# State space layer of a two-block model: where power zero of the output matrices comes from, and which engine flips the coefficients

## The reference, cut to what matters

```python
def s5_mixer(xn, w_in, lam_re, lam_im, b_re, b_im, c_re, c_im, d_skip, log_dt, w_glu):
    u = xn @ w_in                                  # 512 x 1024, in 64 groups of 16
    lam, dt = complex(lam_re, lam_im), exp(log_dt)[:, None]
    a_bar = exp(lam * dt)                          # (64 groups, 64 states)
    b_bar = ((a_bar - 1.0) / lam)[..., None] * complex(b_re, b_im)
    c_mat = complex(c_re, c_im)                    # (64 groups, 16 outputs, 64 states)
    # for every group: s[t] = a_bar * s[t-1] + b_bar @ u[t];  y[t] = real(c_mat @ s[t])
    y = y + d_skip * u
    g = gelu(y)
    val, gate = split(g @ w_glu, 2)
    return val * sigmoid(gate)
```

## Time and profile before

| | us |
|---|---|
| median of 3 runs | 2036.3 (2035.78 to 2037.21) |
| profiled execution, its own time | 2034.78 |
| its span in the trace | 2033.0 |
| PE busy | 1966.4 (97%) |
| DVE busy | 1381.4 (68%) |
| ACT busy | 865.5 (43%) |
| POOL busy | 253.9 (12%) |

### The profile page before, as it was taken

One profiled execution on the slowest core, in us unless ns is written; L12 is line 12 of the kernel. 1 busy time (PEld: TensorE's weight loads), 2 busy tenths in 40 slices (PEclk: granted clock), 3 DMA queues, 4 the chain that ended last, 5 costly groups with the idle time before them and its releaser, 6 DMA issues.

```text
span 2033.0 us, 24999 instructions
## 1 busy us (share of the span) xinstructions
PE 1966.4 (97%) x9434; PEld 1559.6 (77%) x9434; DVE 1381.4 (68%) x2046; ACT 865.5 (43%) x1342; POOL 253.9 (12%) x231
## 2 busy tenths in 40 slices
PE   7999999999999999999999999898999998999997
PEld 5787888888888776788888887687777776876665
DVE  7996476546645449657635654988888888437986
ACT  4574243222233348643222323444443444236773
POOL 3040100000010000010000001233333332000002
PEclk9999999999999999999999999999999999999999
DMA  7455323232233220032233223221222213322012
GB/s 225 109 140 151 100 85 105 81 114 94 85 103 105 92 85 10 5 107 86 84 108 107 93 78 94 83 63 52 78 84 73 80 61 101 96 82 72 28 32 78
DMA packets 79623, 178.33 MB, mean 88 GB/s; under 512 B 17680, under 2 KB 31248, under 8 KB 79504
## 3 DMA queue, kind: packets, MB, share of 16 engines
q1 hardware_dynamic: 75792, 169.92, 27.2%
q0 software_dynamic: 3424, 6.23, 1.2%
q10 hardware_dynamic: 288, 0.59, 0.1%
HBM read 169.43 MB, written 7.27 MB: 87 GB/s over the span
## 4 chain that ended last, share of the span: by engine, by line
PE 70%; DVE 18%; ACT 5%; issue 5%; DMA 1%; SPq 0%; POOL 0%; DVEq 0%; POOLq 0%; ACTq 0%
PE psum L430 16%; PE psum L433 16%; PE psum L431 16%; DVE wl L401 2%; PE psum L471 2%; PE psum L474 2%; PE psum L472 2%; PE psum L855 1%; PE psum L857 1%; PE psum L856 1%; ACT wh L390 1%; PE psum L452 1%; DVE mE L1654 1%; PE psum L455 1%; DVE mE L1673 1%
## 5 line engine op out<-in xcount | busy, mean ns | idle before, releaser
L401 DVE TENSOR_TENSOR wl<-raw,wh 128x1024 fp32r<-128x1024 f32 (+3 forms) x337 | 391.9, 1165 | 326.9 <-ACT wh L390 326.4
L430 PE MATMUL psum<-xh,wh 128*128 128x512 f32 x1368 | 541.6, 396 | 1.3 <-DVE mbc L1531 0.9
L433 PE MATMUL psum<-xh,wl 128*128 128x512 f32 x1368 | 533.7, 390 | 1.3 <-DVE wl L401 1.3
L431 PE MATMUL psum<-xl,wh 128*128 128x512 f32 x1368 | 532.9, 390 | 0.0
L390 ACT ACTIVATE wh<-raw 128x1024 fp32r<-128x1024 f32 (+3 forms) x337 | 315.5, 938 | 272.9 <-PE psum L433 168.5
L430 PEld LDWEIGHTS psum<-xh,wh 128*128 128x128 f32 x1368 | 257.0, 188 | 61.5 <-DVE mbc L1531 3.4
L433 PEld LDWEIGHTS psum<-xh,wl 128*128 128x128 f32 x1368 | 256.8, 188 | 56.7 <-DVE wl L401 2.9
L431 PEld LDWEIGHTS psum<-xl,wh 128*128 128x128 f32 x1368 | 257.0, 188 | 55.1 <-issue 2.6
L578 POOL TENSOR_TENSOR rs<-rs,sq 128x512 f32<-128x512 f32 x41 | 54.2, 1322 | 1087.8 <-ACT sq L563 1087.6
L431 PE MATMUL psum<-fl,wh 128*128 128x512 f32 x352 | 137.0, 389 | 0.0
L433 PE MATMUL psum<-fh,wl 128*128 128x512 f32 x352 | 137.0, 389 | 0.0
(11 more groups left out here) (500 smaller groups left out, 3355.4 us busy)
## 6 DMA issues: line engine op xcount, KB each, us to landing
raw<-d_w SPq DMA_DIRECT2D x224, 512.0 KB, 3.5
raw<-d_w SPq DMA_DIRECT2D x32, 384.0 KB, 3.1
raw<-d_w SPq DMA_DIRECT2D x48, 256.0 KB, 2.6
raw<-d_w SPq DMA_DIRECT2D x32, 320.0 KB, 2.9
Mt<-d_kd SPq DMA_DIRECT2D x64, 64.0 KB, 2.4
bc<-d_bc SPq DMA_DIRECT2D x8, 256.0 KB, 3.3
d_ud<-ust SPq DMA_DIRECT2D x8, 256.0 KB, 3.2
U<-d_ud POOLq DMA_DIRECT2D x64, 32.0 KB, 2.9
```

The lines of the kernel that those rows point to most:

```text
L401: dve.e.tensor_tensor(K.wl[n % NH][:, 0:COLS[n]], K.raw[n % RAW][:, 0:COLS[n]], K.wh[n % NH][:, 0:COLS[n]].bitcast(F32), ALU.subtract).the ...
L430: pe.e.matmul(b[:, :], WH[:, o:o + P], XH, start=(k == k0), stop=False)
L431: pe.e.matmul(b[:, :], WH[:, o:o + P], XL, start=False, stop=False)
L433: mm = pe.e.matmul(b[:, :], WL[:, o:o + P], XH, start=False, stop=(k == k1 - 1))
```

## The change

Three things are edited, all in the S5 layer.

1. **Power zero by DMA.** `combine(q, 1)` makes only powers 1 to 8 (8 lags of 16 columns in place of 9, columns 16 to 143 of `CA`). Columns 0 to 15 are loaded straight from the output matrices in HBM: `load_bc_sp` issues two more DMAs in every round (64 partitions x 8 groups x 16 floats each), on the same semaphore, whose target goes from 16 to 48. The near part waits for them too.
2. **Signs.** So that power zero needs no sign, the imaginary halves change sign throughout: the flips' signs, and `turn` and `mturn` exchanged in the two permutation matmuls.
3. **Flips on ScalarE.** Both flips leave VectorE (prep steps 6 and 7) and are done by ScalarE at step "prep 6", four activations each, the second behind the first, with a part of `CA[2]` as the spare. They start when VectorE has finished `cb` (semaphore `pd` at 5); `combine` waits for them (`pa` at 8 for `cb`, 9 for `pw`).

```diff
-def first_mul(K, dve, out, x, y, t):
+def first_mul(K, dve, out, x, y, t, last=None):
...
-    own(K, dve, "dve", e.tensor_tensor(out[1], out[1], t[1], ALU.add))
-
-
-def flip(K, dve, z, n, s0, s1):
-
-    e = dve.e
-    keep = K.Bs[UP, 0:5, :].rearrange("p a b -> p (a b)")[:, 0:G5 * n].rearrange("p (g k) -> p g k", k=n)
-    own(K, dve, "dve", e.tensor_copy(keep, z[UP, 0, :, :]))
-    own(K, dve, "dve", e.tensor_scalar(z[UP, 0, :, :], z[UP, 1, :, :], s0, None, ALU.mult))
-    own(K, dve, "dve", e.tensor_scalar(z[UP, 1, :, :], keep, s1, None, ALU.mult))
-    own(K, dve, "dve", e.tensor_scalar(z[LOW, 1, :, :], z[LOW, 1, :, :], -1.0, None, ALU.mult))
+    end = e.tensor_tensor(out[1], out[1], t[1], ALU.add)
+    if last:
+        end.then_inc(K.S[last], 1)
+    else:
+        own(K, dve, "dve", end)
+
+
+def flip(K, act, z, n, sign):
+
+    keep = K.CA[2][UP, :, 16:16 + 8 * n].rearrange("p a (j k) -> p a j k", k=n)
+    real, imag = (z[UP, c, :, :].rearrange("p (a j) k -> p a j k", a=8) for c in range(2))
+    own(K, act, "act", act.e.activation(keep, real, ACT.Copy))
+    own(K, act, "act", act.e.activation(real, imag, ACT.Copy, scale=sign))
+    act.e.activation(z[LOW, 1, :, :], z[LOW, 1, :, :], ACT.Copy, scale=-1.0)
+    act.e.activation(imag, keep, ACT.Copy, scale=sign).then_inc(K.S["pa"], 1)
...
@@ prep_act
+    if i == 6:
+        act.wait_ge("pd", 5)
+        flip(K, act, K.cb, 8, -1.0)
+        act.wait_ge("pa", 8)
+        flip(K, act, K.pw, 9, 1.0)
@@ prep_dve
-        first_mul(K, dve, (cb[:, 0], cb[:, 1]), (pw[:, 0, :, 0:8], pw[:, 1, :, 0:8]), b8, t)
-    if i == 6:
-        dve.wait_ge("kdz", 128)
-        flip(K, dve, cb, 8, 1.0, 1.0)
+        first_mul(K, dve, (cb[:, 0], cb[:, 1]), (pw[:, 0, :, 0:8], pw[:, 1, :, 0:8]), b8, t, "pd")
     if i == 7:
-        dve.wait_ge("mat", 1)
         e.memset(K.quarter[:, :], math.pi / 2).then_inc(K.S["prep"], 1)
-        flip(K, dve, pw, 9, -1.0, -1.0)
...
@@ combine
-    c, n, b, dst = (K.cb, 8, 0, K.Bp) if i == 0 else (K.pw, 9, 2, K.CA[q % 3])
-    sh = [P, W, n, 16]
+    c, k, b, dst = (K.cb, 0, 0, K.Bp) if i == 0 else (K.pw, 1, 2, K.CA[q % 3])
+    sh = [P, W, 8, 16]
-    dve.wait_ge(f"bc{q % 3}", 16 * (q // 3 + 1))
+    dve.wait_ge(f"bc{q % 3}", 48 * (q // 3 + 1))
     dve.wait_ge("mat", 2 * q + i)
+    dve.wait_ge("kdz", 128)
+    dve.wait_ge("pa", 8 + i)
...
@@ near_pe
     pe.wait_ge("mat", 2 * q + 2)
+    pe.wait_ge(f"bc{q % 3}", 48 * (q // 3 + 1))
@@ load_bc_sp
     sp.e.dma_start(K.bc[q % 3][:, :, :, :], K.d["bc5"][:, :, GS[q], :]).then_inc(K.S[f"bc{q % 3}"], 16)
+    if q > 2:
+        sp.wait_ge("Kp", q - 2)
+    for half, c in ((LOW, 2), (UP, 3)):
+        sp.e.dma_start(K.CA[q % 3][half, :, 0:16], K.d["bc5"][half, c, GS[q], :]).then_inc(K.S[f"bc{q % 3}"], 16)
@@ swap_pe: K.five("mturn") -> K.five("turn");  state_pe: K.five("turn") -> K.five("mturn")
@@ angles_made: 7 + q if q < 2 else 5 + 2 * q -> 7 + 3 * q if q < 2 else 7 + 2 * q
@@ s5_act
         elif what == "prep" and q == 4:
             angles_act(K, act, 0)
+        elif what == "prep" and q == 6:
+            prep_act(K, act, 6)
```

More of the change, by code:

```diff
@@ L2077, in prep_dve, with by_lag @@
         b8 = [s(j).unsqueeze(2).broadcast_to([P, G5, 8]) for j in (11, 0)]
-        first_mul(K, dve, (cb[:, 0], cb[:, 1]), (pw[:, 0, :, 0:8], pw[:, 1, :, 0:8]), b8, t)
-    if i == 6:
-        dve.wait_ge("kdz", 128)
-        flip(K, dve, cb, 8, 1.0, 1.0)
+        first_mul(K, dve, (cb[:, 0], cb[:, 1]), (pw[:, 0, :, 0:8], pw[:, 1, :, 0:8]), b8, t, "pd")
     if i == 7:
-        dve.wait_ge("mat", 1)
         e.memset(K.quarter[:, :], math.pi / 2).then_inc(K.S["prep"], 1)
-        flip(K, dve, pw, 9, -1.0, -1.0)
-def by_lag(t, n):
-    return t[:, :, 0:n * 16].rearrange("p g (k h) -> p g k h", h=16)
+def by_lag(t, k):
+    return t[:, :, k * 16:(k + 8) * 16].rearrange("p g (k h) -> p g k h", h=16)
 def combine(K, dve, q, i):
-    c, n, b, dst = (K.cb, 8, 0, K.Bp) if i == 0 else (K.pw, 9, 2, K.CA[q % 3])
-    sh = [P, W, n, 16]
+    c, k, b, dst = (K.cb, 0, 0, K.Bp) if i == 0 else (K.pw, 1, 2, K.CA[q % 3])
+    sh = [P, W, 8, 16]
     bc = K.bc[q % 3]
-    dve.wait_ge(f"bc{q % 3}", 16 * (q // 3 + 1))
+    dve.wait_ge(f"bc{q % 3}", 48 * (q // 3 + 1))
     dve.wait_ge("mat", 2 * q + i)
-    dve.e.tensor_tensor(by_lag(K.Bs, n), c[:, 0, GS[q], 0:n].unsqueeze(3).broadcast_to(sh),
+    dve.wait_ge("kdz", 128)
+    dve.wait_ge("pa", 8 + i)
+    dve.e.tensor_tensor(by_lag(K.Bs, 0), c[:, 0, GS[q], k:k + 8].unsqueeze(3).broadcast_to(sh),
                         bc[:, b].unsqueeze(2).broadcast_to(sh), ALU.mult).then_inc(K.S["dve"], dve.up())
@@ L2104, in combine @@
         dve.wait_ge("Yp", q - 2)
-    own(K, dve, "dve", dve.e.tensor_tensor(by_lag(dst, n), c[:, 1, GS[q], 0:n].unsqueeze(3).broadcast_to(sh),
+    own(K, dve, "dve", dve.e.tensor_tensor(by_lag(dst, k), c[:, 1, GS[q], k:k + 8].unsqueeze(3).broadcast_to(sh),
                                            bc[:, b + 1].unsqueeze(2).broadcast_to(sh), ALU.mult))
-    dve.e.tensor_tensor(by_lag(dst, n), by_lag(dst, n), by_lag(K.Bs, n), ALU.add).then_inc(K.S["mat"], 1)
+    dve.e.tensor_tensor(by_lag(dst, k), by_lag(dst, k), by_lag(K.Bs, 0), ALU.add).then_inc(K.S["mat"], 1)
 def busy_pe(K, pe, bank, n):
@@ L2195, in angles_made @@
 def angles_made(q):
-    return 7 + q if q < 2 else 5 + 2 * q
+    return 7 + 3 * q if q < 2 else 7 + 2 * q
 def angles_act(K, act, q):
@@ L2257, in swap_pe @@
     pe.wait_ge("V", q + 1)
-    pe.e.matmul(K.bank[7][:, :], K.five("mturn"), flat(K.V[q % 2]), start=True, stop=True).then_inc(K.S["turned"], 1)
+    pe.e.matmul(K.bank[7][:, :], K.five("turn"), flat(K.V[q % 2]), start=True, stop=True).then_inc(K.S["turned"], 1)
 def scan_dve(K, dve, q):
@@ L2281, in state_pe @@
     pe.wait_ge("S", q + 1)
-    pe.e.matmul(K.bank[0][:, :], K.five("turn"), flat(K.Ss), start=True, stop=True).then_inc(K.S["turned"], 1)
+    pe.e.matmul(K.bank[0][:, :], K.five("mturn"), flat(K.Ss), start=True, stop=True).then_inc(K.S["turned"], 1)
 def state_dve(K, dve, q):
```

## The result

In the same batch of twelve runs each, the kernel before took 2037.16 us (2034.16 to 2039.98) and the changed kernel 2040.72 us (2037.02 to 2043.71): +3.56 us by the medians, ratio 1.002, 95% interval 1.0013 to 1.0027. A second batch gave 2037.56 and 2039.61, ratio 1.0008, 0.9999 to 1.0017, an interval that just includes no difference. So it is slower by some 0.1 to 0.2%. The profiled executions, 2034.78 us before and 2037.02 after (span 2035.1), differ by 2.24; each lies low among its own runs, and 2037.02 is the lowest of the changed kernel's twelve.

What follows compares the result with a forecast made beforehand. TensorE's own list was taken as the bound from 94 to 129 us, VectorE early and in the last rounds. 2.43 - 0.52 + 1.6 - 0.4 - 0.4 + 0.4 + 1.1 - 0.4 = +3.8, giving 2040.1 us, range 2036.0 to 2042.8.

Steps and rivals of the forecast that it cites:

- The split and the gap: Round 0: flips on ScalarE start VectorE's low split of unit 6 2.43 us later; TensorE idles 2.64 us before the transposes.
- the step taken as independent: ScalarE's flips: one activation in each needs nothing of its predecessor and starts 0.53 us after it.
- the working's last term for pw: ScalarE's second flip: the last of its four added times, 0.58 us, bringing its end to 48.97.
- Near 0 and combine(1, 0): Rounds 0 and 1: near 0 comes 1.91 us late after 0.52 of slack; combine(1, 0) waits for it, +1.91.
- The split of round 2: VectorE's split at 81.32 waits for ScalarE, whose list there begins when near 1 ends, so it takes TensorE's +3.5 us.
- The clock: TensorE after round 0's gap: granted clock falls to 0.50 for 3.4 us, costing +1.6 us, bounds 0 and 1.7.
- a clock that holds at 1.00: Sign that the forecast is wrong; it expected 0.50 for some 3 us after TensorE's gap before round 0's transposes.
- +1.6 us, on TensorE, on the path: Clock step, round 0: 3.2 of 3.4 us at half clock hit work on the path to near 0, half lost.
- rival A: Round 0: the stall is there but the clock stays up; +2.2 us, 2038.5 us; chance 0.20.
- Rounds 1 to 6: Combines for CA save 0.4 us each, counted in rounds 1, 2 and 6; in 3 to 5 only read waits shorten.
- SP and post load 1: Round 7: two added DMA issues on SP delay the store of use 7 and post load 1, +1.1 us, bounds 0 and 6.6.
- The end: After the recurrence: a shift at the end of round 7 passes to the end of the kernel one for one.

Runs made afterwards that it cites:

- e1_order: The changed kernel with ScalarE's flips moved behind the high split of weight unit 6: 2036.17 us against 2036.38 for the kernel before, ratio 1.0001.
- e3_flips_only: The kernel before with only the two flips moved to ScalarE, old signs, no added DMAs: 2041.03 us, ratio 1.002 to the kernel before.
- e0_changed: The changed kernel, unaltered, run again in the second batch: 2039.61 us, ratio 1.0008 to the kernel before.
- e7_gap: The kernel before with two fillers in BUSY_TURN[0] instead of five, opening a gap before round 0's transposes: 2038.94 us, ratio 1.0004.
- e5_filler: The changed kernel with eight fillers in BUSY_TURN[0] instead of five, filling the gap before round 0's transposes: 2040.16 us, ratio 1.001 to the kernel before.
- e4_dma_only: The changed kernel with the flips back on VectorE, leaving power zero by DMA and the signs: 2037.1 us, ratio 0.9997 to the kernel before.
- e11_changed_filled: The changed kernel with eight fillers before round 0's transposes and three before round 7's last read: 2037.12 us, ratio 1.0003 to the kernel before.
- e8_before: The kernel before, unedited, run once more in the third batch to see its waits at the last read: 2037.0 us.
- e10_before_filled: The kernel before with three fillers instead of one before round 7's last read: 2035.55 us, ratio 0.9993 to the kernel before.
- e6_fewer_fillers: e2_order_defer with three fillers instead of five before round 0's transposes: 2034.35 us, ratio 0.9981 to the kernel before.
- e9_best: e6_fewer_fillers with three fillers instead of one before round 7's last read: 2031.56 us against 2037.24 for the kernel before, ratio 0.9977.
- e2_order_defer: e1_order with round 7's two small DMAs issued behind the store of use 7: 2035.36 us, ratio 0.999 to the kernel before.

## Why the prediction was right, point by point

**The split and the gap: right.** The low split was put at 50.06 and started at 50.14, after an idle 4.85 us; the transposes were put at 54.87 and started between 54.81 and 54.95 in every profile with this order. The times met, but in part by luck. The eight activations took 5.46 us (43.59 to 49.05) where 5.14 was worked out: the dependent steps are right (0.67 for cb, 0.72 for pw), the step taken as independent starts 0.64 and not 0.53 us after its predecessor, and the working's last term for pw should have been 0.68 by its own rule, not 0.58. Against that, VectorE ended the coefficients 0.23 us earlier in this execution than before (42.87 against 43.10). `e1_order` shows that this order is the cause: with nothing else changed the transposes don't wait and the loss is gone. `e3_flips_only` shows that it alone is enough.

**Near 0 and combine(1, 0): right.** +1.91 was worked out without a fall, +1.92 was found, with the wait of 2.17 at the instruction named. The split of round 2 follows near 1 with the same +1.91.

**The clock: right in kind and in size, wrong as a constant.** The prediction named a clock that holds at 1.00 as a sign of being wrong, and in the first profile of the changed kernel it held. The fall occurs in three of the four profiles with an open gap of 2.9 to 3.6 us here (`e0_changed`, `e3_flips_only`, `e7_gap`) and not in the first of the changed kernel. The step that failed is "+1.6 us, on TensorE, on the path": it is a price of some executions. Where the fall came it cost 1.6 to 1.7 us up to near 0, as worked out. The profiled execution without it came out at +2.24, where rival A had +2.2, so for that execution rival A was the better account. By the Trainium skill, "TensorE: Matmul & The Clock Gate", section "Why this matters for your kernels", gaps of 1.4 to 2.5 us would pass without a fall. The trace disagrees: the gaps of 2.45 and 2.40 us in the kernel before were followed by one, and 1.44 us was enough at the last read of `e3_flips_only`. Nor does the length alone decide: the gap of 2.92 in `e7_gap` was followed by a fall, the gap of 2.93 in the changed kernel was not. Whether the mean loss at round 0 is nearer to 0 or to 1.6 stays open: `e5_filler` was expected to win it back and didn't measurably, and the mean granted clocks of that batch speak for the lower end.

**Rounds 1 to 6: right.** combine's instructions for CA take 1.22 us instead of 1.35, VectorE still waits for reads (2.08 before the scan of round 3), and `e4_dma_only`, which has this saving, doesn't measurably gain from it.

**SP and post load 1: right place, term too small.** The two small issues took 1.31 us where 1.1 was taken, and the wait at post load 1 grew from 0.17 to 2.00. The shift grows there from 1.48 (the scan of round 4) to 3.31. Step by step: the issue of the loads is 1.63 late, the store 3.01, POOL's second half 2.43, and its data land 0.88 us slower (4.55 instead of 3.67). The same growth from the scan of round 4 to post load 1 is 1.19 to 2.16 us in the six profiles with the two DMAs ahead of that store (the changed kernel, `e0_changed`, `e1_order`, `e4_dma_only`, `e5_filler`, `e11_changed_filled`), and 0.08 to 0.21 in three without them (`e3_flips_only`, `e8_before`, `e10_before_filled`). So the DMAs' part is 1.0 to 2.1 us, 1.5 on average, inside the bounds of 0 and 6.6. It took away what `e1_order` had gained up to there. With the two behind the store the growth is -0.07, 0.53 and 1.05 (`e6_fewer_fillers`, `e9_best`, `e2_order_defer`), so their place on SP explains 1.2 of the 1.5 on average, near the 1.1 taken. The rest wasn't tested. One candidate, which the prediction had at nothing: the 32 KB stores of Y land in 2.6 to 2.9 us (medians) in all nine profiles with the small DMAs, and in 2.2 to 2.4 in the five without. The short runs that the Trainium skill, "DMA: Bandwidth & Descriptors", section "Specifications", puts below line rate (under 512 bytes) may be so here: 32 KB in runs of 64 bytes landed in 3.0 us, 256 KB in 3.2, and 64 KB of `Mt` on the same queue in 2.4. No run has these 32 KB in longer runs, so what the run's length costs isn't shown.

**The end: not one for one.** The shift of 2.91 at round 7 grew to 3.63 at the last read and was 2.45 at the end of the layer. The last read waits for `Mt` in some executions of both kernels (2.00 us in `e8_before`, 1.26 in the changed kernel), which adds to a shift and can add a fall; the wait of 1.67 us behind the recurrence then takes some of it away. So `e8_before` ends the layer at 259.36, 1.72 us later than the first profile of the same kernel and 0.73 before the changed one. The prediction did not see this place at all, because the profile of before had only short waits at the read; it is also where part of the spread between runs may come from (2.4 us instead of 6.1 in `e10_before_filled`, but 4.3 and 5.3 in `e11_changed_filled` and `e9_best` with the same fillers, so this isn't settled).

The sum of +3.8 met +3.56, but that closeness is luck: the clock's term was too steady, the DMAs' term about 0.4 too low, the shift did not pass one for one, and the other batch gave 2.05. With both gaps filled the change costs 1.6 to 2.0 (`e11_changed_filled` against `e10_before_filled`); how much of the rest is clock isn't resolved.

## What to carry to other kernels

Before work is moved to an idle engine, look at what stands behind it in that engine's list and who waits for that: ScalarE's busy share of 43% said nothing of the split that VectorE now started 2.5 us late. Fillers cap what an earlier start can bring, so they must be retuned with the schedule. Between single profiles of one kernel the same instruction can stand 1 to 2 us apart, so a shift of that size is to be read against a neighbour in the same profile. Run the parts of a change one by one: here the position of one step cost as much as the whole change, and moving it brought the time back to that of the kernel before. To get below it took two more steps, since the small DMAs and the fillers had held back the gain.

## What the runs showed of the hardware

- Waits of TensorE from 1.44 us on (for `Mt`) were followed by some 7 to 10 us at 0.50 in some executions (1.44, 1.63, 1.91, 1.99, 2.73, 2.75) and not in others (1.26, 1.32, 1.51, 2.00): the length alone doesn't decide.
- A fall after a gap of 2.9 to 3.6 us in dense work cost 1.6 to 1.7 us up to near 0 (9.85 to 9.89 us from the transposes instead of 8.17 to 8.24).
- A 32 KB load in 64-byte runs cost about as much here as a 256 KB load: about 0.65 us of SP's queue each (1.31 for two) against 0.57, and 3.0 against 3.2 us to land.
- At the start of the program the same pair held SP for 7.58 us (from 6.83), and the first weights behind it were issued at 20.64 instead of 14.50, with no effect that the later timeline shows. The short runs don't explain this hold: in the kernel before three 256 KB loads at the same place held SP for 8.08 us (from 6.38).
